# A decoder layer in float32 on one core: GpSimd's low parts in operations of 256 columns, and two additions of one product made as one

## The chip, the core and the metric

The kernel runs on one core of one Trainium2 chip. The time is the device time of one execution in microseconds (us); of several runs the median is given. TensorE (PE in the profile) multiplies, VectorE (DVE), ScalarE (ACT) and GpSimd (POOL) do the elementwise work, and SyncE (SP) issues the loads.

## The reference

One layer over 528 tokens (16 meta tokens and 512 others) of width 1024, all in float32: a half-step SwiGLU FFN, a mixer of gated linear attention and sparse attention, and a second FFN. What the change touches are the two FFNs:

```python
def swiglu(h, w_gate, w_up, w_down):
    return (jax.nn.silu(h @ w_gate) * (h @ w_up)) @ w_down

h = h + 0.5 * swiglu(rmsnorm(h, ffn1_norm[layer]), ffn1_w_gate[layer], ffn1_w_up[layer], ffn1_w_down[layer])
```

D_FF is 2816, that is 22 tiles of 128.

## The kernel before, in words

**Split operands.** Every float32 operand of a matmul is split into a high part, rounded to the type fp32r by ScalarE, and a low part, which is the operand less its high part. A product is made of three matmuls: high by high, high by low, low by high. Weights come by DMA into a ring of four slots (`raw`, 1024 columns each); ScalarE writes the high part (`wh`, `wxh`), and GpSimd or VectorE the low part (`wl`, `wxl`) as a `tensor_tensor` subtraction of two operands in SBUF.

**Seven products.** An FFN's first four tiles are computed plainly. The other 18 are done in steps, each a product of a pair of weight tiles (gate or up) with the tokens, cut in two halves each way and made with seven half-size products in place of eight (Winograd's form of Strassen's method). A step takes two loads (units u and u + 1, halves w11, w12 and w21, w22). For it VectorE makes four sums of weight halves (`sums`, L2056 to L2061, 512 columns each, into `ws` or `wxs`) and two low parts (`low_pair`: L2067 for w22, 512 columns, and L2071 for s3 and s4, 1024 columns). GpSimd makes two low parts (`lo_pair`: L1756 for w11 and w12, and L1761 for s2 and s1, 1024 columns each). TensorE then makes the seven products in the order of `SEVEN` (L2344, 12 matmuls each, of 264 columns in the first FFN and of 256 in the second, whose last 512 tokens alone are needed). The steps alternate: an even step is of the gate, an odd one of the up weights, and what both leave in `t01` and `ubuf` are multiplied into the activations, whose parts are `ah` and `al`. Even and odd steps use different places for their operands (`wh` and `wxh`, `ws` and `wxs`), so a period of the work is two steps.

**The additions.** VectorE adds the products, as they come out of PSUM, into four quarters of `t01` or `ubuf` (L2170 to L2188). A semaphore, `c_add`, counts seven additions a step; `READ_BY` says after how many of them each product's PSUM bank may be written again.

**Downs.** The 18 tiles are in five groups: two tiles, then four times four. While the steps of a group run, the down products of the group before are made between them, two a step: after three of the seven products and at the step's end (L2253 in `step_down`, 12 matmuls of 512 columns in the second FFN, or of 2 x 264 in the first, over four tiles; 6 for the group of two). Both use the one pair of banks 6 and 7, and VectorE adds them to `h` (`add_down`, L2108), after which the bank is free. The weight unit of each down is split by ScalarE and, in `lo` (L1749), by GpSimd: 512 columns, or 256 for the group of two tiles.

**What sets the order.** Each engine has a list of its own, written out by hand, and waits for counts of semaphores. GpSimd's in a step is: the low parts for the next step's pair (L1756, L1761), then those of two downs (L1749). VectorE's is: sums for the next step, additions of products 1 and 2 (counted from 0), low parts for the next step, the first down's addition to h, the additions of products 3 to 6, in an odd step the multiplications L2185 and L2192 and the low parts of the activations (L2083), and the second down's addition to h. SyncE loads a unit when GpSimd and VectorE are through with the unit four before it.

Of the kernel before, what the change touches and what calls it, by code (L numbers as in the profile page):

```python
# [207 lines left out]
def build(nc, x, meta, ffn1, ffn2, mix_norm, w_in, w_a2, b_a, head_norm, w_out, final_norm,  # L208
          cos_t, sin_t, out):
    ctx = ExitStack()  # L210
    with ctx:
# [128 lines left out]

        SEVEN = [("w11", "x11"), ("s2", "t2"), ("s3", "t3"), ("s1", "t1"), ("w12", "x21"), ("w22", "t4"), ("s4", "x22")]

        READ_BY = [0, 1, 2, 4, 5, 6, 7]

        def seven_bank(u, i):

# [1391 lines left out]
        @block.gpsimd  # L1738
        def _(pool):
            pool.memset(ident[:, :], 0.0).then_inc(c_zero, 1)  # L1740
            pool.memset(ones[:, :], 1.0).then_inc(consts, 1)
            pool.wait_ge(c_zero, 1)
            pool.affine_select(out=ident[:, :], in_=ident[:, :], compare_op=ALU.not_equal, fill=1.0, base=0,
                               pattern=[[-1, P]], channel_multiplier=1).then_inc(consts, 1)

            def lo(u):
                n, c = WIDTH[u], -(-WIDTH[u] // HALF_UNIT)
                pool.wait_ge(w_hi, Q_HI[u])
                pool.tensor_tensor(places(1, PLACE[u], c)[:, 0:n], raw[:, u % RING, 0:n],  # L1749
                                   places(0, PLACE[u], c)[:, 0:n].bitcast(F32), ALU.subtract).then_inc(w_split, c)  # L1750

            def lo_pair(u):

                at_p, q = operand_places(u), Q_HI[u] - 7
                pool.wait_ge(w_hi, q + 2)
                pool.tensor_tensor(places(1, at_p["w11"], 2), raw[:, u % RING, :],  # L1756
                                   places(0, at_p["w11"], 2).bitcast(F32), ALU.subtract).then_inc(w_split, 2)

                pool.wait_ge(s_done, 4 * (PAIR_N[u] + 1))
                pool.wait_ge(w_hi, q + 5)  # L1760
                pool.tensor_tensor(places(1, at_p["s2"], 2), places(2, at_p["s2"], 2), places(0, at_p["s2"], 2).bitcast(F32),  # L1761
                                   ALU.subtract).then_inc(w_split, 2)

            def ffn(u0, number, first):

                for v in range(first, 2 * PLAIN):
                    lo(u0 + v)
                for d in range(KT):
                    lo(U_DOWN[number, 0, d])
                for g, (_, cnt) in enumerate(GROUPS):  # L1770
                    for m in range(cnt if g else 0):
                        lo_pair(U_PAIR[number, g, m])
                        for e in range(2 if g > 1 else 0):
                            lo(U_DOWN[number, g - 1, 2 * m + e])
                for d in range(KT):
                    lo(U_DOWN[number, len(GROUPS) - 1, d])

            pool.memset(tri[:, :], 0.0).then_inc(c_zero, 1)
            lo(0)
            pool.wait_ge(c_zero, 2)  # L1780
            pool.affine_select(out=tri[:, :], in_=tri[:, :], compare_op=ALU.is_ge, fill=NEG, base=0,
                               pattern=[[-1, P]], channel_multiplier=1).then_inc(consts, 1)

            steps = 0
            for n, s in enumerate(LEVELS):
                lo(1 + n)
                scratch = xb[:, 0, 0:P]
                blk = scratch.rearrange("p (m a b) -> p m a b", a=2, b=s)
                if n:
                    pool.wait_ge(lv_step, steps)  # L1790
                pool.memset(scratch, 0.0).then_inc(lv_step, 1)
                steps += 1
                pool.wait_ge(lv_step, steps)
                pool.memset(blk[:, :, 1, :], 1.0).then_inc(lv_step, 1)
                steps += 1
                pool.wait_ge(lv_step, steps)

                pool.affine_select(out=blk[:, :, 1, :], in_=blk[:, :, 1, :], compare_op=ALU.is_ge, fill=0.0,
                                   base=0, pattern=[[-2 * s, P // (2 * s)], [0, s]],
                                   channel_multiplier=1).then_inc(lv_step, 1)  # L1800
                steps += 1
                pool.wait_ge(lv_step, steps)

                pool.affine_select(out=blk[:, :, 1, :], in_=blk[:, :, 1, :], compare_op=ALU.is_ge, fill=0.0,
                                   base=s - 1, pattern=[[2 * s, P // (2 * s)], [0, s]],
                                   channel_multiplier=-1).then_inc(lv_step, 1)
                steps += 1
                pool.wait_ge(lv_step, steps)
                pool.tensor_copy(lvm[:, n, :], scratch).then_inc(lv_step, 1)
                steps += 1  # L1810

            ffn(U_FFN1, 0, 1 + len(LEVELS))
            for m in range(6):
                lo(U_MIX + m)

            pool.wait_ge(h_done, H_OUT)
            for m in range(6, M_DQK):
                lo(U_MIX + m)
            for n in range(3):
                lo(U_MIX + M_DQK + n)  # L1820

            for n in range(8):
                lo(U_MIX + M_DQK + 3 + n)
                pool.wait_ge(swapped[5 + n], 64)
                c = META if n < 4 else 0
                s, r = sw[:, n % 4, c:], pjb[:, n, c:]
                pool.tensor_tensor(s, s, sinr[:, c:], ALU.mult).then_inc(q_sin, 1)
                pool.tensor_tensor(r, r, cosr[:, c:], ALU.mult).then_inc(q_cos, 1)
                pool.wait_ge(q_sin, n + 1)
                pool.wait_ge(q_cos, n + 1)  # L1830
                pool.tensor_tensor(r, r, s, ALU.add).then_inc(q_roped, 1)
            lo(U_MIX + M_DV + 3)
            lo(U_MIX + M_GQK)
            lo(U_MIX + M_GQK + 1)
            lo(U_MIX + M_GQK + 2)
            lo(U_MIX + M_GQK + 3)
            for m in range(4):
                lo(U_MIX + M_GR + m)
            lo(U_OUT)
            lo(U_OUT + 1)  # L1840

            pool.wait_ge(lv_x, 2 * (NLV - 1))
            for n in range(2, KT):
                lo(U_OUT + n)
            ffn(U_FFN2, 1, 0)
# [3 lines left out]
        def _(act):  # L1849
# [37 lines left out]
            def ffn(u0, number, norm):  # L1887
# [44 lines left out]
                for (g, m), after in zip(steps, steps[1:] + [None]):  # L1932
# [9 lines left out]
                        hi(U_DOWN[number, last, 0])  # L1942
                    act.wait_ge(w_used, pair_used(v, 0))
                    if n >= 2:
                        act.wait_ge(c_add, 7 * (n - 1))
                    act.activation(pbuf[:, up, 0:w], ps[:, seven_bank(v, 0), 0:w], ACT.Copy).then_inc(p1_kept, 1)
                    if after:
                        hi_w(w_next, 1)
# [7 lines left out]
                    for e in range(2):  # L1956
# [1 line left out]
                            act.wait_ge(t_prod, 2 * it + e + 1)  # L1958
                            high(ubuf[:, 1 - e, 0:2 * w], A_TILE[g] + m - e)
                        else:  # L1960
                            act.wait_ge(c_add, 7 * n + 6 + e)
                            act.activation(t01[:, 1 - e, 0:2 * w], t01[:, 1 - e, 0:2 * w], ACT.Silu).then_inc(g_silu, 1)
                for d in range(3, KT - 1):
                    hi(U_DOWN[number, last, d])
# [46 lines left out]
        def _(dve):  # L2011
# [62 lines left out]
            def ffn(u0, number, norm):  # L2074
# [79 lines left out]
                for (g, m), after in zip(steps, steps[1:] + [None]):  # L2154
                    v, up = U_PAIR[number, g, m], m % 2
                    n = PAIR_N[v]
                    it, c = n // 2, 7 * n
                    buf, p1 = (ubuf if up else t01), pbuf[:, up, 0:w]
                    first, second = (slice(e * w, (e + 1) * w) for e in range(2))

                    def product_of(i):
# [12 lines left out]
                        low_pair(U_PAIR[(number, *after)])  # L2174
                    if g > 1:
                        add_down(g - 1, 2 * m)
                    dve.tensor_tensor(buf[:, 0, second], product_of(3), buf[:, 0, second], ALU.add).then_inc(c_add, 1)
                    dve.wait_ge(c_add, c + 2)
                    dve.tensor_tensor(buf[:, 1, second], product_of(3), buf[:, 1, first], ALU.add).then_inc(c_add, 1)
                    dve.tensor_tensor(buf[:, 0, first], product_of(4), p1, ALU.add).then_inc(c_add, 1)  # L2180
                    dve.tensor_tensor(buf[:, 1, first], product_of(5), buf[:, 1, first], ALU.add).then_inc(c_add, 1)  # L2181
                    if up:
                        dve.wait_ge(c_add, c + 6)
                        dve.wait_ge(g_silu, 2 * it + 1)
                        dve.tensor_tensor(ubuf[:, 1, 0:2 * w], ubuf[:, 1, 0:2 * w], t01[:, 1, 0:2 * w],  # L2185
                                          ALU.mult).then_inc(t_prod, 1)
                    dve.wait_ge(c_add, c + 3)
                    dve.tensor_tensor(buf[:, 0, second], product_of(6), buf[:, 0, second], ALU.add).then_inc(c_add, 1)  # L2188
                    if up:
                        dve.wait_ge(c_add, c + 7)  # L2190
                        dve.wait_ge(g_silu, 2 * it + 2)
                        dve.tensor_tensor(ubuf[:, 0, 0:2 * w], ubuf[:, 0, 0:2 * w], t01[:, 0, 0:2 * w],  # L2192
                                          ALU.mult).then_inc(t_prod, 1)
# [45 lines left out]
        def _(pe):  # L2239
# [35 lines left out]
            def ffn(u0, number, norm):  # L2275
# [45 lines left out]
                for g in range(1, last + 1):  # L2321
                    for m in range(GROUPS[g][1]):
# [3 lines left out]
                        for i, (wn, xn_) in enumerate(SEVEN):  # L2326
# [11 lines left out]
                            elif (g, m) == (1, 0):  # L2338
                                pe.wait_ge(h_done, hd + 5 + i // 2)
                            else:  # L2340
                                pe.wait_ge(c_add, 7 * (n - 1) + READ_BY[i + 1])
                            for k in range(KT // 2):
                                for c, (lo, xlo) in enumerate(((0, 0), (0, 1), (1, 0))):
                                    mm = pe.matmul(ps[:, seven_bank(v, i), 0:w], places(lo, at_p[wn], 1)[:, k * P:(k + 1) * P],  # L2344
# [7 lines left out]
                for k0, k1, ds in ((0, 2, range(3)), (2, cnt, range(3)), (0, cnt, range(3, KT))):  # L2352
                    for d in ds:
                        v = U_DOWN[number, last, d]
                        if k0 == 0:
                            pe.wait_ge(w_split, Q_END[v])
                            if 1 <= d < 4:
                                pe.wait_ge(c_add, 7 * (n + 1))
                            else:
                                pe.wait_ge(h_done, hd + KT * last + (d - 3 if d else 0))  # L2360
                        down(v, down_bank(last, d), order[last], norm, k0, k1, ft + GROUPS[last][0] if d == 0 else None)
# [77 lines left out]
```

## Time and profile before

| | us |
|---|---|
| median of three runs | 1127.38 |
| lowest and highest | 1127.23, 1129.89 |
| the profiled execution | 1126.08 |
| its span | 1124.4 |

| engine | busy us | share of the span | instructions |
|---|---|---|---|
| TensorE, matmuls | 1054.5 | 94% | 7399 |
| VectorE | 922.0 | 82% | 1298 |
| ScalarE | 461.3 | 41% | 736 |
| GpSimd | 503.3 | 45% | 289 |

The time of the whole execution is 1.7 us more than the span, which begins with the first recorded instruction and ends with the last. An engine's busy time holds what it waits inside an instruction, for a port for instance; a wait for a semaphore is idle time. Matmuls are pipelined, so the times of single ones overlap, and the pace is read from start to start. L with a number is a line of the kernel; one line can stand for many operations, and `(+1 forms)` means that a row holds another shape as well.

### The profile page before, as it was taken

What the parts mean: (1) busy time and instruction counts of PE and PEld (TensorE: products, weight loads), DVE (VectorE), ACT (ScalarE), POOL (GpSimd) and SP (SyncE); (2) the same over time, 40 slices, a digit from 0 to 9 for tenths busy, and PEclk for the clock granted to TensorE, in tenths of its full rate; (3) what the DMA queues carried; (4) which work ended last, traced back from release to release, by engine and by line L of the source; (5) the groups of instructions that cost most, each with busy time, mean ns of one, the idle gap of its engine ahead of it and who ended that gap; (6) DMA issues with size and microseconds to landing.
All of it is one profiled execution on the core that took longest, in us unless ns stands there. A gap on an engine that the chain in (4) does not pass through costs nothing. (4 is left out here: it accounts for less than half of the span.)

```text
span 1124.4 us, 19157 instructions
## 1 busy us (share of the span) xinstructions
PE 1054.5 (94%) x7399; PEld 949.0 (84%) x7399; DVE 922.0 (82%) x1298; ACT 461.3 (41%) x736; POOL 503.3 (45%) x289
## 2 busy tenths in 40 slices
PE   6999898999999979999999999999889899999997
PEld 6999898999999978789767777877688788888986
DVE  6889999899999458699776595578899999999945
ACT  5444333433433254372255526443434333433325
POOL 3744545455544435159721203334554445544530
PEclk8999899999999989999999999999999999999999
DMA  6223333333243324434321102211423433333221
GB/s 190 67 67 103 94 95 92 88 104 101 79 112 86 104 74 129 109 85 124 94 57 39 49 10 76 75 57 47 122 57 95 113 103 85 94 105 103 75 76 75
DMA packets 172254, 98.67 MB, mean 88 GB/s; under 512 B 6787, under 2 KB 167606, under 8 KB 172166
## 3 DMA queue, kind: packets, MB, share of 16 engines
q1 hardware_dynamic: 172166, 97.47, 31.3%
q8 instruction: 59, 0.97, 0.4%
q14 instruction: 29, 0.24, 0.1%
HBM read 91.18 MB, written 2.10 MB: 83 GB/s over the span
## 5 line engine op out<-in xcount | busy, mean ns | idle before, releaser
L1749 POOL TENSOR_TENSOR wl<-raw,wh 128x1024 fp32r<-128x1024 f32 (+1 forms) x65 | 147.5, 2281 | 270.1 <-ACT wh L1857 232.2
L1749 POOL TENSOR_TENSOR wxl<-raw,wxh 128x512 fp32r<-128x512 f32 (+1 forms) x84 | 128.4, 1532 | 223.9 <-ACT wxh L1857 223.9
L2253 PE MATMUL ps<-ah,wxh 128*128 128x264 f32 (+1 forms) x456 | 126.4, 332 | 37.8 <-DVE h L2108 31.9
L2253 PE MATMUL ps<-xh,wh 128*128 128x264 f32 (+3 forms) x416 | 123.3, 343 | 12.3 <-issue 6.4
L2253 PE MATMUL ps<-ah,wxl 128*128 128x264 f32 (+1 forms) x456 | 124.0, 327 | 0.0
L2253 PE MATMUL ps<-al,wxh 128*128 128x264 f32 (+1 forms) x456 | 123.6, 326 | 0.0
L2253 PEld LDWEIGHTS ps<-ah,wxh 128*128 128x128 f32 x456 | 77.2, 193 | 50.4 <-issue 39.8
L2253 PE MATMUL ps<-xl,wh 128*128 128x264 f32 (+3 forms) x416 | 118.2, 331 | 0.0
L2253 PE MATMUL ps<-xh,wl 128*128 128x264 f32 (+3 forms) x416 | 117.8, 330 | 0.0
L2344 PE MATMUL ps<-xh,wh 128*128 128x264 f32 (+1 forms) x360 | 102.0, 283 | 1.8 <-DVE h L2108 1.8
L2344 PE MATMUL ps<-xl,wh 128*128 128x264 f32 (+1 forms) x360 | 101.6, 282 | 0.0
L2344 PE MATMUL ps<-xh,wl 128*128 128x264 f32 (+1 forms) x360 | 101.6, 282 | 0.0
L2108 DVE SCALAR_TENSOR_TENSOR h<-ps,h 128x528 f32<-128x528 f32 (+1 forms) x96 | 65.7, 691 | 42.0 <-PE ps L2253 41.8
L2067 DVE TENSOR_TENSOR wl<-raw,wh 128x512 fp32r<-128x512 f32 x36 | 99.5, 2763 | 0.0
L2253 PEld LDWEIGHTS ps<-xh,wh 128*128 128x128 f32 (+1 forms) x416 | 71.4, 191 | 29.3 <-issue 21.3
L2253 PEld LDWEIGHTS ps<-ah,wxl 128*128 128x128 f32 x456 | 77.5, 193 | 6.7
L2253 PEld LDWEIGHTS ps<-al,wxh 128*128 128x128 f32 x456 | 77.4, 192 | 5.2
L1894 ACT ACTIVATE ah<-ubuf 128x528 fp32r<-128x528 f32 (+1 forms) x36 | 23.0, 640 | 132.0 <-DVE ubuf L2185 123.3
L2253 PEld LDWEIGHTS ps<-xh,wl 128*128 128x128 f32 (+1 forms) x416 | 71.4, 191 | 6.3
L2253 PEld LDWEIGHTS ps<-xl,wh 128*128 128x128 f32 (+1 forms) x416 | 71.4, 191 | 4.8 <-issue 0.2
L2344 PEld LDWEIGHTS ps<-xh,wh 128*128 128x128 f32 x360 | 67.8, 188 | 2.5 <-DVE wl L2071 2.2
L1857 ACT ACTIVATE wh<-raw 128x1024 fp32r<-128x1024 f32 (+1 forms) x65 | 61.5, 971 | 19.4 <-PE ps L536 15.6
(293 smaller groups left out, 3060.3 us busy)
## 6 DMA issues: line engine op xcount, KB each, us to landing
raw<-in_ffn_w_gate SPq DMA_DIRECT2D x44, 512.0 KB, 4.1
raw<-in_ffn_w_up SPq DMA_DIRECT2D x44, 512.0 KB, 4.1
raw<-in_ffn_w_down SPq DMA_DIRECT2D x80, 256.0 KB, 2.8
raw<-in_w_in SPq DMA_DIRECT2D x28, 512.0 KB, 4.0
raw<-in_w_out SPq DMA_DIRECT2D x8, 512.0 KB, 3.4
xin<-in_x SPq DMA_DIRECT2D x4, 512.0 KB, 4.5
raw<-in_ffn_w_down SPq DMA_DIRECT2D x16, 128.0 KB, 3.1
out<-xin SPq DMA_DIRECT2D x4, 512.0 KB, 3.6
```

The lines of the kernel that those rows point to most:

```text
L1749: pool.tensor_tensor(places(1, PLACE[u], c)[:, 0:n], raw[:, u % RING, 0:n], places(0, PLACE[u], c)[:, 0:n].bitcast(F32), ALU.subtract).the ...
L1857: act.activation(places(0, PLACE[u], c)[:, 0:n], raw[:, slot, 0:n], ACT.Copy).then_inc(w_hi, c)
L1894: act.activation(ah[:, j, tk], src, ACT.Copy).then_inc(a_hi, 1)
L2067: dve.tensor_tensor(places(1, at_p["w22"], 1), raw[:, (u + 1) % RING, HALF_UNIT:UNIT], places(0, at_p["w22"], 1).bitcast(F32), ALU.subtrac ...
L2108: dve.scalar_tensor_tensor(out=as_parts(h[:, d, tk], norm), in0=psum_parts(bank, norm), scalar=0.5, in1=as_parts(h[:, d, tk], norm), op0=A ...
L2253: mm = pe.matmul(ps[0:m, bank + a, 0:width], places(lo, PLACE[u], -(-WIDTH[u] // HALF_UNIT))[:, k * P:k * P + m], r[:, tile, t:t + width], ...
L2344: mm = pe.matmul(ps[:, seven_bank(v, i), 0:w], places(lo, at_p[wn], 1)[:, k * P:(k + 1) * P], x_operand(xlo, xn_, w)[:, k, :], start=(k == ...
```

## The change

GpSimd's three kinds of low parts go through a helper, `low`, that makes them in pieces of 256 columns. Only the last piece counts up `w_split`, by as much as the one operation did. That is so everywhere in the kernel, in the mixer too.

The additions of product 3 into two quarters (L2177 and L2179) become one, which reads the product twice by a repeated dimension and takes as its other operand the two quarters that lie one behind the other in memory, `[0, second]` and `[1, first]`. It waits for the addition of product 2 (`c_add` at c + 2). The counts of `c_add` go from seven to six a step, with `READ_BY` and the waits adapted, and product 5's addition now waits for the merged one.

```diff
-        READ_BY = [0, 1, 2, 4, 5, 6, 7]
+        READ_BY = [0, 1, 2, 3, 4, 5, 6]
...
+            SHORT = 2 * P
+
+            def low(dst, src, high, counts):
+
+                for c in range(0, counts * HALF_UNIT, SHORT):
+                    if c < src.shape[-1]:
+                        part = slice(c, c + SHORT)
+                        op = pool.tensor_tensor(dst[:, part], src[:, part], high[:, part].bitcast(F32), ALU.subtract)
+                op.then_inc(w_split, counts)
+
             def lo(u):
                 n, c = WIDTH[u], -(-WIDTH[u] // HALF_UNIT)
                 pool.wait_ge(w_hi, Q_HI[u])
-                pool.tensor_tensor(places(1, PLACE[u], c)[:, 0:n], raw[:, u % RING, 0:n],
-                                   places(0, PLACE[u], c)[:, 0:n].bitcast(F32), ALU.subtract).then_inc(w_split, c)
+                low(places(1, PLACE[u], c), raw[:, u % RING, 0:n], places(0, PLACE[u], c), c)
...
                 pool.wait_ge(w_hi, q + 2)
-                pool.tensor_tensor(places(1, at_p["w11"], 2), raw[:, u % RING, :],
-                                   places(0, at_p["w11"], 2).bitcast(F32), ALU.subtract).then_inc(w_split, 2)
+                low(places(1, at_p["w11"], 2), raw[:, u % RING, :], places(0, at_p["w11"], 2), 2)
 
                 pool.wait_ge(s_done, 4 * (PAIR_N[u] + 1))
                 pool.wait_ge(w_hi, q + 5)
-                pool.tensor_tensor(places(1, at_p["s2"], 2), places(2, at_p["s2"], 2), places(0, at_p["s2"], 2).bitcast(F32),
-                                   ALU.subtract).then_inc(w_split, 2)
+                low(places(1, at_p["s2"], 2), places(2, at_p["s2"], 2), places(0, at_p["s2"], 2), 2)
...
-                    it, c = n // 2, 7 * n
-                    buf, p1 = (ubuf if up else t01), pbuf[:, up, 0:w]
+                    it, c = n // 2, 6 * n
+                    buf, p1 = (ubuf if up else t01)[:, :, :], pbuf[:, up, 0:w]
...
-                    dve.tensor_tensor(buf[:, 0, second], product_of(3), buf[:, 0, second], ALU.add).then_inc(c_add, 1)
+
                     dve.wait_ge(c_add, c + 2)
-                    dve.tensor_tensor(buf[:, 1, second], product_of(3), buf[:, 1, first], ALU.add).then_inc(c_add, 1)
+                    two = buf.rearrange("p f n -> p (f n)")[:, w:2 * TOK - w].rearrange("p (f n) -> p f n", f=2)[:, :, 0:w]
+                    dve.tensor_tensor(buf[:, :, second], product_of(3).unsqueeze(1).broadcast_to([P, 2, w]), two,
+                                      ALU.add).then_inc(c_add, 1)
                     dve.tensor_tensor(buf[:, 0, first], product_of(4), p1, ALU.add).then_inc(c_add, 1)
+                    dve.wait_ge(c_add, c + 3)
                     dve.tensor_tensor(buf[:, 1, first], product_of(5), buf[:, 1, first], ALU.add).then_inc(c_add, 1)
                     if up:
-                        dve.wait_ge(c_add, c + 6)
+                        dve.wait_ge(c_add, c + 5)
...
-                    dve.wait_ge(c_add, c + 3)
                     dve.tensor_tensor(buf[:, 0, second], product_of(6), buf[:, 0, second], ALU.add).then_inc(c_add, 1)
```

GpSimd's list in one step of four-tile groups, before (the names are output, then inputs; the waits are those that the instruction itself carries):

```order
L1749 TENSOR_TENSOR wxl<-raw,wxh 128x512 [waits w_hi] x2
L1756 TENSOR_TENSOR wxl<-raw,wxh 128x1024 [waits w_hi]
L1761 TENSOR_TENSOR wxl<-wxs,wxh 128x1024 [waits w_hi,s_done]
L1749 TENSOR_TENSOR wxl<-raw,wxh 128x512 [waits w_hi] x2
```

and the same place after the change:

```order
L1754 TENSOR_TENSOR wxl<-raw,wxh 128x256 [waits w_hi]
L1754 TENSOR_TENSOR wxl<-raw,wxh 128x256
L1754 TENSOR_TENSOR wxl<-raw,wxh 128x256 [waits w_hi]
L1754 TENSOR_TENSOR wxl<-raw,wxh 128x256
L1754 TENSOR_TENSOR wxl<-raw,wxh 128x256 [waits w_hi]
L1754 TENSOR_TENSOR wxl<-raw,wxh 128x256 x3
L1754 TENSOR_TENSOR wxl<-wxs,wxh 128x256 [waits w_hi,s_done]
L1754 TENSOR_TENSOR wxl<-wxs,wxh 128x256 x3
```

Nothing changes its place; of each operation's pieces only the first carries a wait.

VectorE's list from the low parts of an odd step to the first multiplication, before:

```order
L2067 TENSOR_TENSOR wl<-raw,wh 128x512 [waits w_hi]
L2071 TENSOR_TENSOR wl<-ws,wh 128x1024 [waits s_done,w_hi]
L2108 SCALAR_TENSOR_TENSOR h<-ps,h 128x528 [waits h_done,w_used]
L2177 TENSOR_TENSOR ubuf<-ps,ubuf 128x264 [waits w_used]
L2179 TENSOR_TENSOR ubuf<-ps,ubuf 128x264 [waits w_used,c_add]
L2180 TENSOR_TENSOR ubuf<-ps,pbuf 128x264 [waits w_used]
L2181 TENSOR_TENSOR ubuf<-ps,ubuf 128x264 [waits w_used]
L2185 TENSOR_TENSOR ubuf<-ubuf,t 128x528 [waits g_silu,c_add]
```

and after it:

```order
L2075 TENSOR_TENSOR wl<-raw,wh 128x512 [waits w_hi]
L2079 TENSOR_TENSOR wl<-ws,wh 128x1024 [waits s_done,w_hi]
L2116 SCALAR_TENSOR_TENSOR h<-ps,h 128x528 [waits h_done,w_used]
L2188 TENSOR_TENSOR ubuf<-ps,ubuf 128x2x264 [waits w_used,c_add]
L2190 TENSOR_TENSOR ubuf<-ps,pbuf 128x264 [waits w_used]
L2192 TENSOR_TENSOR ubuf<-ps,ubuf 128x264 [waits w_used,c_add]
L2196 TENSOR_TENSOR ubuf<-ubuf,t 128x528 [waits g_silu,c_add]
```

The two additions of product 3 are one row, and the wait for `c_add` has moved from the second of them to it and to product 5's addition. Lines are eight to eleven further down in the changed kernel.

## Rows read from the trace of the kernel before

**Rows 1.** The page: the span.

```profile
span 1124.4 us, 19157 instructions
```

**Rows 2.** The waits of TensorE: total us, times, longest.

```profile
PE ps L2253 <- DVE h L2108: 31.9, 26, 4.4
```

**Rows 3.** Matmuls of L2344, first and last start, in each FFN.

```profile
L2344 PE MATMUL ps<-xqh,wh x108: 279/283/288, 95.0 to 361.5; 128*128 128x264 f32 x108
L2344 PE MATMUL ps<-xqh,wxl x108: 278/283/425, 106.5 to 378.6; 128*128 128x264 f32 x108
...
L2344 PE MATMUL ps<-xqh,wh x108: 276/279/415, 806.7 to 1069.3; 128*128 128x256 f32 x108
L2344 PE MATMUL ps<-xqh,wxl x108: 278/280/416, 818.1 to 1086.3; 128*128 128x256 f32 x108
```

**Rows 4.** The chain that ended last: start, us, what; two dense runs of matmuls.

```profile
1080.84 5.70 PE ps L2344 x48
...
1090.16 22.50 PE ps L2253 x96
```

**Rows 5.** Busy time in one period: PE, PEld, DVE, ACT, POOL, clock, DMA.

```profile
960.41:993.29 32.88, 31.52 (x218) 29.03 (x217) 31.08 (x36) 12.12 (x19) 16.82 (x9) 1.00 0.36 97
```

**Rows 6.** VectorE in order of time in that period: start, us, operation.

```profile
960.33 1.20 DVE L2056 TENSOR_TENSOR wxs<-raw 128x512 f32<-128x512 f32 x1
...
965.58 0.41 DVE L2170 TENSOR_TENSOR t<-ps,pbuf 128x256 f32<-128x256 f32 x1
...
966.37 2.84 DVE L2067 TENSOR_TENSOR wl<-raw,wh 128x512 fp32r<-128x512 f32 x1
969.14 2.31 DVE L2071 TENSOR_TENSOR wxl<-wxs,wxh 128x1024 fp32r<-128x1024 f32 x1
971.37 0.68 DVE L2108 SCALAR_TENSOR_TENSOR h<-ps,h 128x512 f32<-128x512 f32 x1
971.98 0.41 DVE L2177 TENSOR_TENSOR t<-ps,t 128x256 f32<-128x256 f32 x1
...
975.87 0.68 DVE L2056 TENSOR_TENSOR ws<-raw 128x512 f32<-128x512 f32 x1
...
981.71 0.42 DVE L2170 TENSOR_TENSOR ubuf<-ps,pbuf 128x256 f32<-128x256 f32 x1
```

**Rows 7.** GpSimd in order of time in the same period.

```profile
966.26 2.41 POOL L1761 TENSOR_TENSOR wxl<-wxs,wxh 128x1024 fp32r<-128x1024 f32 x1 [2.47 <-ACT wxh L1875]
968.63 1.74 POOL L1749 TENSOR_TENSOR wxl<-raw,wxh 128x512 fp32r<-128x512 f32 x1
```

**Rows 8.** GpSimd in order of time: 1024, 256 and 512 columns, undisturbed.

```profile
29.20 2.35 POOL L1749 TENSOR_TENSOR wl<-raw,wh 128x1024 fp32r<-128x1024 f32 x1 [7.17 <-ACT wh L1857]
...
136.97 0.74 POOL L1749 TENSOR_TENSOR wxl<-raw,wxh 128x256 fp32r<-128x256 f32 x1 [5.41 <-ACT wxh L1857]
...
509.97 1.29 POOL L1828 TENSOR_TENSOR pjb<-pjb,cs 128x512 f32<-128x512 f32 x1
```

**Rows 9.** VectorE: the additions to h that end two even steps, group of two tiles.

```profile
136.42 0.71 DVE L2108 SCALAR_TENSOR_TENSOR h<-ps,h 128x528 f32<-128x528 f32 x1 [1.47 <-PE ps L2253]
...
165.88 0.71 DVE L2108 SCALAR_TENSOR_TENSOR h<-ps,h 128x528 f32<-128x528 f32 x1 [0.18 <-PE ps L2253]
```

**Rows 10.** Five microseconds after a wait of TensorE: columns as in rows 5.

```profile
135.00:140.00 5.00, 5.00 (x27) 5.00 (x26) 3.58 (x3) 3.10 (x6) 2.75 (x2) 0.57 0.39 99
```

**Rows 11.** VectorE and GpSimd in the mixer, in order of time.

```profile
513.03 3.50 DVE L1337 TENSOR_SCALAR mask<-mask 100x228 f32<-100x228 f32 x2
516.45 1.20 DVE L1327 MAX8 small<-mask 100x8 f32<-100x428 f32 x2
...
515.02 1.32 POOL L1827 TENSOR_TENSOR sw<-sw,cs 128x512 f32<-128x512 f32 x1
516.31 1.38 POOL L1828 TENSOR_TENSOR pjb<-pjb,cs 128x512 f32<-128x512 f32 x1
```

More of the change, by code:

```diff
@@ L1944, in ffn @@
                     if n >= 2:
-                        act.wait_ge(c_add, 7 * (n - 1))
+                        act.wait_ge(c_add, 6 * (n - 1))
                     act.activation(pbuf[:, up, 0:w], ps[:, seven_bank(v, 0), 0:w], ACT.Copy).then_inc(p1_kept, 1)
@@ L1960, in ffn @@
                         else:
-                            act.wait_ge(c_add, 7 * n + 6 + e)
+                            act.wait_ge(c_add, 6 * n + 5 + e)
                             act.activation(t01[:, 1 - e, 0:2 * w], t01[:, 1 - e, 0:2 * w], ACT.Silu).then_inc(g_silu, 1)
@@ L2186, in ffn @@
                                           ALU.mult).then_inc(t_prod, 1)
-                    dve.wait_ge(c_add, c + 3)
                     dve.tensor_tensor(buf[:, 0, second], product_of(6), buf[:, 0, second], ALU.add).then_inc(c_add, 1)
                     if up:
-                        dve.wait_ge(c_add, c + 7)
+                        dve.wait_ge(c_add, c + 6)
                         dve.wait_ge(g_silu, 2 * it + 2)
@@ L2340, in ffn @@
                             else:
-                                pe.wait_ge(c_add, 7 * (n - 1) + READ_BY[i + 1])
+                                pe.wait_ge(c_add, 6 * (n - 1) + READ_BY[i + 1])
                             for k in range(KT // 2):
@@ L2357, in ffn @@
                             if 1 <= d < 4:
-                                pe.wait_ge(c_add, 7 * (n + 1))
+                                pe.wait_ge(c_add, 6 * (n + 1))
                             else:
```

## The prediction, made before the changed kernel ran

> **What bounds the kernel now.** I read the page first, then the waits of TensorE, then the extent and the pace of its matmuls in the two stages of seven products, then one period of those stages on VectorE and GpSimd, operation by operation. The profiled execution took 1126.1 us around a span of 1124.4 us [rows 1]; it lies 1.3 us below the median of the runs (1127.4), which is nothing beside what follows. On the page TensorE looks like the bound. But its longest total wait is for VectorE's addition to h, 31.9 us in 26 waits [rows 2], and these waits lie in the two stages of seven products. There the matmuls of L2344 run from 95.0 to 378.6 us in the first FFN and from 806.7 to 1086.3 us in the second [rows 3]; with the last matmul's 0.1 us that is 283.7 and 279.6 us.
>
> How long would TensorE need without a wait? A stage has 18 steps of seven products with 12 matmuls each, 1512 in all. Between them, up to the last of the seven, stand 8 down products over two tiles (6 matmuls each) and 23 over four (12 each), 324 matmuls. At full pace 48 matmuls of L2344 took 5.70 us (0.119 each) and 96 of L2253 22.50 us (0.234 each) [rows 4]. The second FFN's floor is 1512 x 0.11875 + 324 x 0.2344 = 179.6 + 75.9 = 255.5 us, 24.1 below what it takes. The first FFN has 264 columns for 256; scaled by 528/512 (an upper bound, since not all of a matmul's time goes with its columns) the floor is 263.5 us, 20.2 below. So 44.3 us of the kernel are not TensorE's work, though it is "busy" 94% of the span.
>
> The period of two steps shows whose they are. In the second FFN, between 960.41 and 993.29 us, VectorE is busy 31.1 of 32.9 us [rows 5], while TensorE's own work is 168 x 0.11875 + 48 x 0.2344 = 31.2 us. VectorE's time isn't work: an operation on 512 columns took 0.68 us where nothing disturbed it (L2056 at 975.87), yet L2067, as large, took 2.84 us [rows 6]. GpSimd explains both: its L1761 ran from 966.26 to 968.67, and L2067 ended 0.5 us later; its L1749 then ended 1.2 us after L2067, and L2071 1.1 us after L1749 [rows 6, 7]. The two engines take turns, by whole instructions, whenever both read two operands from SBUF. VectorE waits for up to 1024 columns of GpSimd, and in return GpSimd for one VectorE operation.
>
> **Part one: 256 columns a piece.** 72 operations of the pairs and 53 others go from one to four, 80 of 512 columns to two; 16 of 256 stay. GpSimd gets 455 more instructions. Undisturbed, 1024 columns take 2.35 us and 256 take 0.74 [rows 8], so four pieces cost 2.96, or 0.6 more, if nothing overlaps; in a queue about 0.06 comes off each (the 512 columns of L1749 took 1.23 us from L2067's end to their own [rows 6, 7], 1.29 alone [rows 8]), and I take 0.68 a piece. In a period GpSimd is busy 16.8 of 32.9 us [rows 5] and would rise to some 24 pieces x 0.68 plus its turns of waiting, about 23 us. That stays under 31, so it is hidden in the steady stage.
>
> What VectorE gains, in one period: the four sums now take 965.58 - 960.33 = 5.25 us in one step and 981.71 - 975.87 = 5.84 in the other [rows 6]. With turns of 0.68 for GpSimd and 0.5 for VectorE, four take 4.7 each: 1.7 gained in a period. The two low parts (L2067, L2071) take 971.37 - 966.37 = 5.0 us; after the change 0.68 + 0.5 + 0.68 + 1.08 = 2.9, so 4.2 in a period. VectorE's load drops from 31.1 to 25.2 us, against TensorE's 31.2. TensorE becomes the bound.
>
> In the group with small downs (two tiles) the case is tighter. A period there was 165.88 - 136.42 = 29.5 us [rows 9], TensorE's work is 168 x 0.1225 + 24 x 0.242 = 26.4 at most, and VectorE's about 29.5 - 3.6 = 25.9 (its sums there gain only 0.6, as GpSimd has one short down operation instead of a long one; the low parts 3.0). They are near enough that each will wait for the other at the joints: I leave 1 us a period, 4 in the kernel. TensorE's 4 us wait around 130 us also lowered its granted clock, to 0.57 over the five microseconds behind it [rows 10], that is to the 1.2 GHz level for most of them; some 2 us of work are lost by it on top of the wait. This comes back with the wait, and is inside the 44.3.
>
> Does GpSimd let VectorE in between two pieces that have no semaphore wait between them, as the pieces do? In the steady stage each GpSimd operation has a wait of its own. One place answers: L1828 follows L1827 without a wait. Two VectorE operations of L1337, short when alone, took 3.50 us together and the next began at 516.45; GpSimd's L1827 ended at about 516.3, and L1828 took 1.38 against the 1.29 of an undisturbed one [rows 8, 11]. So the second one went in at the boundary between them. One instance, but the right one.
>
> **Part two: one addition for two.** L2177 and L2179 (256 columns each out of PSUM, 0.41 us, a third of a microsecond from start to start) become one of 512 columns. The nearest row, the addition to h, has 512 columns out of PSUM and takes 0.61 to its successor's start [rows 6]: about 0.05 us saved a step, between nothing and 0.2; at worst, if the repeated read is slow, 0.2 lost. 36 steps, on an engine that is no longer the bound: zero. The new wait for the merged addition before product 5 has product 4's addition ahead of it to cover it. The bank of product 3 is released by the merged addition, as it was by the second of the two. Zero.
>
> **Sum.** 44.3 us above the floor, less 4 for the tight groups, less 2.3 for joints elsewhere (28 steps of less than 0.1): 38 gained. Outside the stages TensorE is dense or waits for ScalarE and weights; longer GpSimd chains there cost up to 1 us at the start of each FFN's downs and the shorter stalls of VectorE give about as much. 1126 - 38 = **1088 us**. Bounds: nothing left over, 1126 - 44 - 4 for openings that gain = 1078; two thirds of it, 1098.
>
> **Rivals.** First, **a new wait takes half**. The pieces lose a turn to each sum: the low part of the next pair, and with it the release of the weight buffer and the next load, comes 6 x 0.68 + 4 x 0.5 = 6.1 us after a step begins where it was about 5. Steps last 13 to 16 us and the load some 4, so there is slack; against it stands that both stages start from idle, where GpSimd is followed closely by TensorE. If each step of the 36 kept 0.5 us, 18 us are lost again: 1106, with a band of 1098 to 1116.
>
> Second, **slower**: GpSimd keeps the ports through a run of pieces. Then VectorE waits as before, but for 2.96 instead of 2.35 us and for 1.48 instead of 1.29 [rows 8]: 4 x 0.61 + 4 x 0.19 = 3.2 us in each of 16 VectorE-bound periods, +51: 1177. It decides as soon as VectorE doesn't get in at a boundary without a wait. The Trainium skill (GPSIMD Engine Reference, "Instruction dispatch") says that each of GpSimd's cores begins the next instruction when its own share is done, with no barrier; by that rule there may be no moment at which all have let go. [Rows 11] speak against it.
>
> Third, **the change doesn't do what it says**: VectorE gets in, but only after two pieces. Then sums take 6 x 0.68 + 4 x 0.5 = 6.1 us, 0.55 more than now on average, and low parts 4 x 0.68 + 1.6 = 4.3, 0.7 less; over a period nothing: 1126.
>
> **How the numbers follow.** The forecast gets 0.72, the first rival 0.17, the second 0.06, the third 0.05. The two first cases are both faster by over 0.3% (3.4 us, about what a measurement of this kernel can tell from no change); of the third, 0.04 is within it. Faster 0.89, same 0.04, slower 0.07. The range of 1078 to 1112 us holds the forecast's case and most of the first rival.
>
> **What would show it.** VectorE's L2067 (now L2075) at about 1.2 us instead of 2.76, its total down from 922 to some 820 us; GpSimd pieces of 0.7 us alone and up to 1.2 in turns, its total up to some 600 or more; TensorE's wait for h under 8 us; the matmuls of the seven products spanning some 266 and 259 us. If L2067's mean stays above 2.5 us with GpSimd's total up, the second rival holds; if VectorE falls and the stages don't shrink, the first.

## The result, and the profile after

The changed kernel takes 1102.2 us (median of 4 runs, 1098.9 to 1103.8) against 1127.3: a ratio of 0.977, 95% interval 0.974 to 0.980. The forecast was 1088, with a range of 1078 to 1112. The direction and the range hold; of the 38 us that the forecast takes off, 25 came.

The page of the changed kernel begins as follows (busy us, share of the span, instructions):

```profile
span 1101.7 us, 19489 instructions
...
PE 1049.0 (95%) x7399; PEld 945.2 (86%) x7399; DVE 795.8 (72%) x1262; ACT 470.3 (43%) x736; POOL 658.4 (60%) x744
```

VectorE has lost 126 us of busy time and GpSimd gained 155. The span is 22.7 us shorter than that of [rows 1] (this profiled execution, 1103.8 us, was the slowest of the four).

One period of the second FFN in the busy-time view, to be laid beside [rows 5], and the same place on VectorE and GpSimd in order of time, beside [rows 6, 7]:

```profile
955.22:986.26 31.04, 31.04 (x217) 28.91 (x217) 25.26 (x32) 12.56 (x18) 23.30 (x24) 1.00 0.38 102
```

```profile
958.04 0.69 DVE L2116 SCALAR_TENSOR_TENSOR h<-ps,h 128x512 f32<-128x512 f32 x1 [2.36 <-PE ps L2263]
959.55 1.25 DVE L2064 TENSOR_TENSOR ws<-raw 128x512 f32<-128x512 f32 x1 [0.82 <-DMA raw<-in_ffn_w_gate]
960.73 1.22 DVE L2065 TENSOR_TENSOR ws<-raw 128x512 f32<-128x512 f32 x1
961.87 1.22 DVE L2067 TENSOR_TENSOR ws<-ws,raw 128x512 f32<-128x512 f32 x1
...
964.17 0.41 DVE L2178 TENSOR_TENSOR ubuf<-ps,pbuf 128x256 f32<-128x256 f32 x1
...
964.96 1.14 DVE L2075 TENSOR_TENSOR wl<-raw,wh 128x512 fp32r<-128x512 f32 x1
966.02 1.75 DVE L2079 TENSOR_TENSOR wl<-ws,wh 128x1024 fp32r<-128x1024 f32 x1
967.69 0.68 DVE L2116 SCALAR_TENSOR_TENSOR h<-ps,h 128x512 f32<-128x512 f32 x1
968.29 0.68 DVE L2188 TENSOR_TENSOR ubuf<-ps,ubuf 128x512 f32<-128x512 f32 x1
968.89 0.41 DVE L2190 TENSOR_TENSOR ubuf<-ps,pbuf 128x256 f32<-128x256 f32 x1
```

```profile
960.20 4.65 POOL L1754 TENSOR_TENSOR wl<-raw,wh 128x256 fp32r<-128x256 f32 x4
964.81 4.25 POOL L1754 TENSOR_TENSOR wl<-ws,wh 128x256 fp32r<-128x256 f32 x4
969.02 1.43 POOL L1754 TENSOR_TENSOR wxl<-raw,wxh 128x256 fp32r<-128x256 f32 x2
```

Here nearly all is as forecast. A period lasts 31.04 us in place of 32.88, and TensorE is busy through the whole of it. VectorE's load is 25.3 us (forecast 25.2, before 31.1), GpSimd's 23.3 (forecast 23). The sums start 1.14 to 1.26 us apart: one turn of VectorE and one piece of GpSimd. Four of them take 4.6 us (959.55 to 964.17), the two low parts 2.7 (964.96 to 967.69); 4.7 and 2.9 were forecast. VectorE now waits for TensorE (2.36 us) and, a thing to be kept in mind, 0.82 us for a load. L2067 of before, now L2075, has a mean of 0.95 us over all its 36 operations (2.76 before, 1.2 forecast). The merged addition takes 0.60 us to its successor's start, where the two took 0.66 (from L2177 at 971.98 [rows 6] to L2180 at 972.64).

The extents of the two stages, beside [rows 3]: first and last start of their matmuls.

```profile
L2354 PE MATMUL ps<-xqh,wh x108: 279/283/288, 97.6 to 351.2; 128*128 128x264 f32 x108
...
L2354 PE MATMUL ps<-xqh,wxl x108: 278/283/289, 108.0 to 367.4; 128*128 128x264 f32 x108
...
L2354 PE MATMUL ps<-xqh,wh x108: 275/280/286, 800.1 to 1047.8; 128*128 128x256 f32 x108
...
L2354 PE MATMUL ps<-xqh,wxl x108: 278/280/286, 810.3 to 1063.6; 128*128 128x256 f32 x108
```

The stages last 269.9 and 263.6 us (283.7 and 279.7 before): 29.9 us gained. The floors of the forecast were 263.5 and 255.5, so 14.5 us are left in them where 6.3 were expected. The waits of the changed kernel name a new one:

```profile
DVE ws L2064 <- DMA raw<-in_ffn_w_gate: 29.8, 13, 4.1
...
PE ps L2263 <- DVE h L2116: 17.5, 11, 3.1
...
DVE wxs L2064 <- DMA raw<-in_ffn_w_up: 10.0, 7, 4.0
```

TensorE still waits 17.5 us for the additions to h (31.9 in [rows 2]; under 8 was forecast), and VectorE waits 40 us for loads of the pairs' weights. In the group with small downs, in order of time on VectorE, then GpSimd, SyncE's queue and TensorE:

```profile
855.42 0.69 DVE L2064 TENSOR_TENSOR wxs<-raw 128x512 f32<-128x512 f32 x1 [1.46 <-issue]
...
862.60 0.68 DVE L2116 SCALAR_TENSOR_TENSOR h<-ps,h 128x512 f32<-128x512 f32 x1
...
865.08 0.69 DVE L2116 SCALAR_TENSOR_TENSOR h<-ps,h 128x512 f32<-128x512 f32 x1 [0.21 <-PE ps L2263]
869.89 0.69 DVE L2064 TENSOR_TENSOR ws<-raw 128x512 f32<-128x512 f32 x1 [4.13 <-DMA raw<-in_ffn_w_gate]
```

```profile
859.70 4.25 POOL L1754 TENSOR_TENSOR wxl<-wxs,wxh 128x256 fp32r<-128x256 f32 x4 [0.70 <-ACT wxh L1883]
```

```profile
863.97 0.99 SPq L1622 DMA_DIRECT2D raw<-in_ffn_w_gate  x2
```

```profile
863.42 0.47 PE L2263 MATMUL ps<-ah,wxh 128*128 128x512 f32 x1 [1.43 <-DVE h L2116]
```

The loads of the next two units are issued at 863.97, when the last piece of GpSimd's second low part (s2 and s1) ends at 863.95, and the sums that need them begin at 869.89. So a step is a loop: the sums, with ScalarE's high part beside the last of them (4.3 us to GpSimd's start at 859.70), four pieces in turns (4.25), the two loads (5.9 from the first issue to the sums that wait for them), in all 14.5 us from 855.42 to 869.89, where TensorE's own work would be 25.6 / 2 = 12.8. TensorE feels it through VectorE's list: the first down's addition to h stands behind the sums and low parts, so it comes late with them (862.60 to 863.28), and TensorE, which needs the bank that it frees, has waited 1.43 us when it goes on at 863.42. The low part of s2 and s1 doesn't read the buffer; the load waits for it because `w_split` is counted at the end of all of a pair's low parts (`Q_END`).

### The profile page after: what moved, and what is told of

Same layout as the page of the kernel before. It is cut to its first block, busy times and chain, and to the rows that moved or that the text cites. A ratio compares the mean times of both kernels' runs of the same rounds, so it can differ in the third digit from the quotient of the medians.

```text
span 1101.7 us, 19489 instructions
## 1 busy us (share of the span) xinstructions
PE 1049.0 (95%) x7399; PEld 945.2 (86%) x7399; DVE 795.8 (72%) x1262; ACT 470.3 (43%) x736; POOL 658.4 (60%) x744
## 3 DMA queue, kind: packets, MB, share of 16 engines
q1 hardware_dynamic: 172166, 97.47, 31.9%
## 4 chain that ended last, share of the span: by engine, by line
PE 46%; POOL 6%; DVE 5%; issue 2%; ACT 2%; DMA 2%; DVEq 0%; SPq 0%; ACTq 0%; POOLq 0%
PE ps L2263 19%; PE ps L2354 12%; PE ps L536 5%; PE ps L550 4%; POOL wl L1754 3%; DMA raw<-in_ffn_w_gate 1%; POOL wxl L1754 1%; PE ps L673 1%; PE ps L717 1%; DMA raw<-in_ffn_w_up 1%; PE ps L696 1%; PE ps L625 1%; POOL pjb L1839 1%; POOL pjb L1836 1%; POOL sw L1835 1%
## 5 line engine op out<-in xcount | busy, mean ns | idle before, releaser
L1754 POOL TENSOR_TENSOR wl<-raw,wh 128x256 fp32r<-128x256 f32 x308 | 258.5, 873 | 260.9 <-ACT wh L1865 205.2
L1754 POOL TENSOR_TENSOR wxl<-raw,wxh 128x256 fp32r<-128x256 f32 x224 | 205.5, 944 | 128.1 <-ACT wxh L1865 121.5
L2263 PE MATMUL ps<-ah,wxh 128*128 128x264 f32 (+1 forms) x456 | 124.4, 327 | 19.6 <-DVE h L2116 17.5
L2263 PE MATMUL ps<-xh,wh 128*128 128x264 f32 (+3 forms) x416 | 124.5, 347 | 14.5 <-POOL wl L1754 7.3
L1754 POOL TENSOR_TENSOR wxl<-wxs,wxh 128x256 fp32r<-128x256 f32 x72 | 76.2, 1088 | 14.6 <-ACT wxh L1883 13.9
L1754 POOL TENSOR_TENSOR wl<-ws,wh 128x256 fp32r<-128x256 f32 x72 | 76.2, 1088 | 11.6 <-ACT wh L1883 11.6
```

The lines of the kernel that those rows point to most:

```text
L1754: op = pool.tensor_tensor(dst[:, part], src[:, part], high[:, part].bitcast(F32), ALU.subtract)
L2263: mm = pe.matmul(ps[0:m, bank + a, 0:width], places(lo, PLACE[u], -(-WIDTH[u] // HALF_UNIT))[:, k * P:k * P + m], r[:, tile, t:t + width], ...
```

## Experiments

For all of them, what a profile shows of the stages, from the first and last starts of their matmuls with 0.1 us for the last one (us; "between" is from the first FFN's last such matmul to the second's first; the 38 us after the second stage are the same in all):

| kernel | first starts | stage 1 | between | stage 2 | median |
|---|---|---|---|---|---|
| before | 95.0 | 283.7 | 428.0 | 279.7 | 1127.3 |
| changed | 97.6 | 269.9 | 432.6 | 263.6 | 1102.2 |
| additions only | 95.4 | 283.6 | 430.4 | 281.2 | 1129.6 |
| pieces only | 95.1 | 269.8 | 429.3 | 265.6 | 1100.3 |
| changed, earlier loads | 94.5 | 262.3 | 429.7 | 255.2 | 1083.4 |
| pieces in pairs only | 95.9 | 269.3 | 429.8 | 265.3 | 1100.1 |
| before, earlier loads | 96.1 | 282.7 | 430.0 | 281.7 | 1129.4 |
| 512 columns, earlier loads | 95.7 | 269.0 | 431.2 | 263.5 | 1098.2 |
| 128 columns, earlier loads | 102.8 | 263.0 | 440.6 | 255.6 | 1100.9 |
| s2 and s1 whole | 95.0 | 272.0 | 432.2 | 264.4 | 1102.5 |
| changed, again | 95.5 | 269.5 | 430.1 | 264.6 | 1099.8 |
| pieces in pairs, earlier loads | 95.2 | 262.5 | 430.9 | 255.2 | 1083.9 |

Each was measured beside the kernel before on its own chip, which took 1128.1 to 1129.4 us there; ratios are to that.

**The merged addition alone.** The changed kernel with whole operations:

```diff
-            SHORT = 2 * P
+            SHORT = UNIT
...
-                        part = slice(c, c + SHORT)
+                        part = slice(c, min(c + SHORT, src.shape[-1]))
```

> The merged addition alone; GpSimd's low parts stay whole (1024, 512 or 256 columns). My theory puts all of the gain on the pieces: this run is within 0.3% of the kernel before (1124 to 1130 us), since at most 0.05 us a step, 2 us in all, come off VectorE. VectorE is still near 920 us busy and L2075 near 2.7 us each. Rival: the merged addition and its shorter chain of waits carry a good part of the 25 us; then this run is below 1118 us.

Measured: 1129.6 us, ratio 1.0005 (0.9995 to 1.0015), VectorE 920.7 us busy. Nothing, as forecast.

**The pieces alone.** The kernel before with `low`, `lo` and `lo_pair` as in the change.

> Pieces of 256 columns alone, with the seven additions of before. My theory: the gain is all here, 1100 to 1104 us, since in the stages VectorE is no longer the bound and some 0.07 us more of it a step are hidden. Rival (the additions matter): above 1108 us.

Measured: 1100.3 us, ratio 0.975 (0.973 to 0.976). The pieces alone give the whole gain.

**Earlier loads.** The changed kernel; only the pairs' units are released sooner:

```diff
                 if u >= RING:
-                    sp.wait_ge(w_split, Q_END[u - RING])
+                    sp.wait_ge(w_split, Q_END[u - RING] - (2 if (u - RING) in PAIR_N or (u - RING - 1) in PAIR_N else 0))
```

> The changed kernel, but the loads of a pair's two units wait only for the low part of w11 and w12 (and, as before, for VectorE's low part of w22), and no more for GpSimd's low part of s2 and s1, which doesn't read the buffer. Theory: in the group with small downs the loop of sums, ScalarE's high parts, GpSimd's four pieces (4.25 us in turns) and the load bounds the step at 14.4 us; without the pieces in it the loop is some 3 us shorter and TensorE's 12.8 to 13.2 us bound the step. 8 such steps: 8 to 12 us gained, 1090 to 1095 us, and VectorE's wait for the loads of gate and up weights falls from 40 to under 15 us. Rival: the loss in these stages is of VectorE and GpSimd taking turns, and the loads only fill what they leave; then the time stays within 3 us of 1102.

Measured: 1083.4 us (1081.8 to 1084.7), ratio 0.960 (0.958 to 0.961): 16 to 19 us less than with the change alone, more than the 8 to 12 that I expected. The first sum's waits for loads are down from 40 us to 4.2, and TensorE's for the additions to h from 17.5 to 4.7 (total, times):

```profile
  DMA raw<-in_ffn_w_gate: 4.2, 4
```

```profile
PE ps L2263 <- DVE h L2116: 4.7, 3, 2.2
```

The extents:

```profile
L2354 PE MATMUL ps<-xqh,wh x108: 279/283/288, 94.5 to 340.4; 128*128 128x264 f32 x108
...
L2354 PE MATMUL ps<-xqh,wxl x108: 278/283/289, 105.0 to 356.7; 128*128 128x264 f32 x108
...
L2354 PE MATMUL ps<-xqh,wh x108: 278/280/286, 786.5 to 1025.9; 128*128 128x256 f32 x108
...
L2354 PE MATMUL ps<-xqh,wxl x108: 278/280/286, 796.7 to 1041.6; 128*128 128x256 f32 x108
```

The stages last 262.3 and 255.2 us: TensorE's floor (forecast 263.5, called an upper bound, and 255.5). In the first FFN TensorE is busy without a gap where the small groups lie, at the full granted clock. The busy-time view of 120 to 180 us, first of the changed kernel, then with earlier loads:

```profile
120.00:180.00 60.00, 54.49 (x444) 53.77 (x443) 46.46 (x65) 24.48 (x37) 40.78 (x41) 1.00 0.39 103
```

```profile
120.00:180.00 60.00, 60.00 (x496) 59.95 (x495) 55.42 (x74) 26.52 (x40) 49.72 (x50) 1.00 0.40 110
```

The loop reaches a little further than the 8 small steps. In the changed kernel TensorE also waits where the downs of four tiles have begun:

```profile
191.17 0.48 PE L2263 MATMUL ps<-ah,wxh 128*128 128x264 f32 x2 [1.12 <-DVE h L2116]
```

And in the second FFN a wait of 3.12 us lowers TensorE's granted clock, to 0.75 over these five microseconds:

```profile
834.61 0.76 PE L2263 MATMUL ps<-ah,wxh 128*128 128x512 f32 x1 [3.12 <-DVE h L2116]
```

```profile
835.00:840.00 5.00, 5.00 (x28) 4.42 (x28) 1.75 (x5) 2.32 (x4) 1.57 (x3) 0.75 0.77 212
```

Over both stages TensorE is idle for 13.5 us in the changed kernel and for 0.7 with the earlier loads. That is 12.8 of the 16.0 us by which the stages differ; the lowered clock is part of the rest.

**Pieces in the pairs only.** `lo` as it was before; `lo_pair` in pieces.

> The changed kernel with only the low parts of the pairs in pieces; those of the plain stages, of the downs and of the mixer are whole again. Theory: outside the two stages of seven products the pieces cost 7 us (the first stage begins 2.6 us later than before, and the stretch between the stages is 4.5 us longer, with GpSimd's pieces on its critical chain in the mixer); they come back, less what VectorE waits for whole downs of 512 columns, which is hidden in the groups of four tiles: 1094 to 1099 us. The stretch from the last matmul of the seven products in the first FFN to the first in the second is 428 us, as before, not 432.6. Rival: those 7 us are scatter of TensorE's granted clock around the stages' ends; then the stretch stays above 431 us.

Measured: 1100.1 us, ratio 0.974 (0.972 to 0.975), and 429.8 us between the stages. The theory missed by a little, and its reason falls: the stretch between is 429 to 431 in most of the profiles, with whole operations (430.4, 430.0) as with pieces (429.3, 429.7). The 428.0 and 432.6 of the first two profiles are its two ends (432.2 comes once more, below). The rival's figure, above 431 us, didn't come either, but its reason finds support: in the 20 us that begin 20 us after the end of stage 1, the granted clock was 0.74 in the first profile of the changed kernel and 0.83 in that of its repetition further below, at the same place of the program (the clock is the third number from the end):

```profile
387.50:407.50 20.00, 13.43 (x81) 13.19 (x80) 11.85 (x17) 9.18 (x13) 7.76 (x10) 0.74 0.23 53
```

```profile
385.00:405.00 20.00, 13.42 (x85) 13.19 (x85) 11.82 (x17) 9.19 (x13) 7.79 (x10) 0.83 0.24 54
```

By an estimate from these two lines (0.09 x 20 us) that is 1.8 of the 2.5 us between their stretches, 432.6 and 430.1. It doesn't explain the 432.2, where the clock of that place was 0.83.

**Whole operations with the earlier loads.** The edit of the earlier loads on the kernel before.

> The kernel before (whole operations, seven additions) with the earlier loads of the pairs' units alone. Theory: the load after GpSimd's last low part bounds a step only once VectorE no longer does; before the change VectorE bounds it, so this edit alone gives under 0.5%: 1122 to 1129 us. Rival: the earlier load is a gain of its own, of some 19 us, that adds to that of the pieces; then 1105 to 1112 us.

Measured: 1129.4 us, ratio 1.0001 (0.998 to 1.002), 0.4 us above the range in microseconds, as the kernel before took 1128.1 on this chip. In its trace the low part of w22 still takes 2.8 us (shortest, median and longest in ns):

```profile
L2067 DVE TENSOR_TENSOR wl<-raw,wh x36: 2098/2821/2840, 93.5 to 1069.2; 128x512 fp32r<-128x512 f32 x36
```

The two gains don't add: the load's loop costs nothing that shows until the pieces have taken VectorE off the path.

**Pieces of 512 columns with the earlier loads** (`SHORT = 4 * P`, and the slice cut at the end as above).

> Pieces of 512 columns with the earlier loads. Theory of turns: GpSimd's turn is 1.23 us for 0.68, so two low parts on VectorE take 4.0 us (3.3 with 256 columns) and four sums up to 5.7 (4.6); VectorE's load is some 28 to 29 us a period, under TensorE's 31 in the groups with downs of four tiles and over its 26 in those of two, where 4 periods lose 2 to 3 us each: 1090 to 1097 us against 1083. Rival: what helps is not the length of the turn but that GpSimd's operation is broken at all; then 1083 us, as with 256.

Measured: 1098.2 us, ratio 0.972 (0.969 to 0.974), 1 us above the range for the theory of turns and far from its rival. A stretch across the small groups of the first FFN, and one of a period's length in the groups of four tiles:

```profile
120.00:180.00 60.00, 56.45 (x449) 55.90 (x448) 57.95 (x66) 24.04 (x39) 38.23 (x27) 0.97 0.36 97
950.00:981.00 31.00, 31.00 (x218) 28.86 (x217) 28.08 (x34) 12.56 (x18) 20.60 (x12) 1.00 0.38 105
```

VectorE's load is 28.1 us a period: hidden under TensorE's 31 there, and nearly full (57.95 of 60) in the small groups, where TensorE waits. The turn's length counts, and only where VectorE is near the bound.

**Pieces of 128 columns with the earlier loads** (`SHORT = P`).

> Pieces of 128 columns with the earlier loads. By the rows for 256, 512 and 1024 columns GpSimd's operation costs 0.2 us and 2.1 ns a column, so 0.43 us in a queue for 128. Theory: TensorE bounds the stages already, so shorter turns give nothing there, and GpSimd has 48 pieces a period, 20.6 us and turns of waiting of 6 to 10 us, close to TensorE's 31 and in the small groups over it: 1084 to 1100 us, never below 1082. Rival: VectorE's turns still cost time; then below 1081 us.

Measured: 1100.9 us, ratio 0.974 (0.972 to 0.976), about a microsecond above the upper end that I gave, and not for the reason that I gave. The stages stay at the floor (263.0 and 255.6 us). The loss lies outside: the first stage starts at 102.8 us, 8 later than with 256 columns, and 440.6 us lie between the stages, 11 more. There GpSimd's low parts are close ahead of TensorE. TensorE's waits for them, over the whole kernel, show a part of the loss (7.4 us with 256 columns); the rest I haven't traced:

```profile
PE ps L2263 <- POOL wl L1754: 12.5, 5, 6.3
```

**The low part of s2 and s1 whole**, all others in pieces, loads as in the change:

```diff
-                low(places(1, at_p["s2"], 2), places(2, at_p["s2"], 2), places(0, at_p["s2"], 2), 2)
+                pool.tensor_tensor(places(1, at_p["s2"], 2), places(2, at_p["s2"], 2), places(0, at_p["s2"], 2).bitcast(F32),
+                                   ALU.subtract).then_inc(w_split, 2)
```

> The changed kernel (late loads) with the low part of s2 and s1 whole again, all others in pieces. Theory of the load loop: that low part is the last thing a load waits for; whole it takes 2.4 us for 4.25 and the load starts 1.8 us earlier, in each of the 8 steps of the small groups and the few others that wait for a load: some 12 to 15 us back from the loop, against VectorE's low parts 1.5 to 2 us longer a step, hidden in the large groups: 1090 to 1099 us. Rival (no such loop, only turns): VectorE gets slower and nothing comes back: 1104 to 1112 us.

Measured: 1102.5 us, ratio 0.976 (0.974 to 0.978). Neither forecast. The loop did get shorter, as its theory says: VectorE waits 5.0 us for the gate weights where it waited 29.8, and in the small groups an even step takes 13.5 us (854.42 to 867.93) for 14.5. But VectorE has the long turn back, and in the odd step, where it also has the activations, it is busy without a gap for 14.9 us (867.93 to 882.81):

```profile
854.42 0.68 DVE L2065 TENSOR_TENSOR wxs<-raw 128x512 f32<-128x512 f32 x1
...
859.26 2.81 DVE L2076 TENSOR_TENSOR wl<-raw,wh 128x512 fp32r<-128x512 f32 x1
...
867.93 0.69 DVE L2065 TENSOR_TENSOR ws<-raw 128x512 f32<-128x512 f32 x1 [1.07 <-DMA raw<-in_ffn_w_gate]
...
882.81 0.68 DVE L2065 TENSOR_TENSOR wxs<-raw 128x512 f32<-128x512 f32 x1
```

```profile
DVE ws L2065 <- DMA raw<-in_ffn_w_gate: 5.0, 9, 1.3
```

So the period of two steps is 28.4 us, where the changed kernel has 29.5 (from its sums at 855.42 to those at 884.91) and TensorE's work is 25.6. The one wait gave way to VectorE's load, and over both stages the time is 2 to 3 us longer than the changed kernel's (272.0 and 264.4 us).

**The changed kernel again**, without an edit.

> The changed kernel once more, beside the version with earlier loads. Its profiled execution had a stretch of 432.6 us between the stages of seven products, where every experiment with 256 or 1024 columns had 429 to 430, and a first stage that began at 97.6 us, where the others had 94.5 to 96. If both are scatter, as I hold after the pairs-only run, this profile shows 429 to 430.5 and 94.5 to 96.5, and 1099 to 1103 us. If they belong to the change, they come again.

Measured: 1099.8 us (1098.3 to 1100.5), ratio 0.974 (0.972 to 0.976); the first stage starts at 95.5 us, and 430.1 lie between. The 97.6 and the 432.6 didn't come again: both were mostly scatter. The stages, 269.5 and 264.6 us, come out as before.

**Pieces in the pairs only, with the earlier loads.**

> Pieces of 256 columns in the pairs' low parts alone, all others whole, with the earlier loads. Theory: the whole 512 columns of the downs at the head of a step cost VectorE's sums one longer turn, and in the small groups they have only 256 columns; TensorE bounds either way, so 1082 to 1086 us, the same as with pieces everywhere. Rival: fewer GpSimd instructions outside the stages give 3 us or more, below 1080 us.

Measured: 1083.9 us, ratio 0.959 (0.957 to 0.961), the same as with pieces everywhere. Of the versions tried these two are the fastest.

## Why the prediction was right or wrong

**What bounds the kernel**: right. VectorE bounded the stages, by its waits for GpSimd's long operations. With whole operations neither of the other two edits gains anything (1.0005, 1.0001); pieces alone bring the gain. The working has one slip: the second stage took 279.7 us, not 279.6, so 44.4 us stood above the floor.

**The turns**: right, to 0.2 us: 1.16 on average for sum and piece (1.18 forecast), 4.6 and 2.7 us for the four sums and the two low parts (4.7 and 2.9). A boundary between two pieces without a wait is enough for VectorE to get in. The second rival (GpSimd keeps the ports through a run) and the third (only after two pieces) are ruled out by these rows. The Trainium skill (GPSIMD Engine Reference, "Instruction dispatch") says that GpSimd's cores go on to the next instruction without a barrier; here that doesn't keep VectorE out, whose sums start 1.14 to 1.26 us apart beside a run of four pieces.

**The groups of four tiles**: right. TensorE bounds them, 31.04 us a period for 31.2 computed.

**The merged addition at zero**: right; 0.06 us a step on an engine that is not the bound.

**The floor of the stages**: right, and reached, but by another kernel: 262.3 and 255.2 us with the earlier loads, 1.5 us under the 519.0 computed.

**The tight groups at 1 us a period and "joints elsewhere" at 2.3 us**: wrong; this is the step that failed. I set VectorE's load against TensorE's and took the rest for slack. The first rival has the right mechanism (the pieces delay the next load, and with it the sums) but puts the release 6.1 us after the step begins and the load at some 4 us, and finds slack. In the trace the release comes 8.5 us after the first sum (855.42 to 863.95) and the sums that wait for the loads start 5.9 us later. The code releases the buffer not where it is last read but after the low part of s2 and s1, which starts only when sums and high part are done and which the pieces stretch from 2.4 to 4.25 us. Sums, pieces and load make a loop of 14.5 us; the forecast never follows that chain from the release to the sums. With the release moved, 269.9 + 263.6 us become 262.3 + 255.2: 16.0 us above what TensorE needs, where the forecast leaves 6.3 us above a floor that it puts 1.5 us too high.

The profiled execution took 1103.8 us, 15.8 above the forecast. Of these, 8.2 lie in the stages (533.5 us for 519.0 + 6.3), and 7.2 outside, in the late start of the first stage (2.6) and the long stretch between (4.6). The repeated run has 8.8 us and 2.6 us there, so some 4.6 us of the second part are scatter.

**The chances**: the outcome lies between the forecast's case and the first rival's, at 1102 for its 1106, and nearer to the rival in time and in cause. The forecast put 0.72 on TensorE as the bound of all steps and 0.17 on that rival. That the time still fell into the range is due to the range, which was made wide enough to hold both cases.

## What to carry to other kernels

Where VectorE reads two operands from SBUF while GpSimd reads there too, each of its operations can wait for a whole GpSimd instruction (2.8 us for an operation of 0.68 here). In this kernel the best cut was the one that makes GpSimd's turn about as long as VectorE's own operation: 512 columns left VectorE near the bound, 256 took it off, and 128 gave nothing more in these stages and cost 19 us outside. Before pricing such a relief, follow what each buffer's release really waits for: the next bound here was a load held back by an operation that doesn't read its buffer, and one line of the release, worth nothing before the change, gave 16 to 19 us after it.

## What the runs showed of the hardware

A GpSimd operation on two operands in SBUF takes, undisturbed, 0.74 us for 256 columns, 1.29 for 512 (a multiplication; the others are subtractions) and 2.35 for 1024 [rows 8]. In the run with pieces of 128 columns, in order of time on GpSimd:

```profile
953.25 1.72 POOL L1754 TENSOR_TENSOR wxl<-raw,wxh 128x128 fp32r<-128x128 f32 x4
```

Four pieces took 1.72 us, 0.43 each. From these rows I estimate some 0.2 us an instruction, whatever its size, and 2.1 ns a column. And a VectorE addition that reads 256 columns of PSUM twice by a repeated dimension runs as fast as one over 512 different columns: 0.60 us to the next start, as the addition to h.
